# Expert weights loaded into the first mixer's own buffers, and normed rows stored from ScalarE's queue

## The chip, the cores and the metric

The kernel runs on one core of one Trainium2 chip. The metric is the device time of one execution in microseconds (us), lower is better; the time of before is the median of 3 runs.

## The reference, cut to what matters

Two layers over 512 latent and 256 context tokens of width 1024, all in float32. Layer 0 mixes by retention and by a gated linear recurrence, layer 1 by latent attention. Each layer then norms and modulates its rows, routes each token to 2 of 32 experts and runs these:

```python
h = modulate(rmsnorm(x, g), shift, scale)
e_flat, weights = router(h)                      # a group of 8 experts, then 2 in it
xin = h[row_tok].reshape(n_blocks, 128, 1024)    # the rows of each expert
yb = (silu(xin @ w_gate[e]) * (xin @ w_up[e])) @ w_down[e]
x = x + gate * y                                 # y: each token's two outputs, weighted and summed
```

An expert's `w_gate`, `w_up` and `w_down` are 2 MB each. All 32 experts' weights are read in each layer, whatever the routing.

## The kernel before, in words

Engines run their own instruction streams and meet on semaphores written out by hand. The program is a row of blocks; each ends with a barrier of all engines. Four stages matter here.

**Input projection** (`ab_project`) and **retention** (`retention`) of layer 0. They fill `rows` (four planes of 6 tiles by 512), `yT` (the recurrence's result, channels on partitions) and use `c.hT`. `retention` loads the output projection's weights into `w`, the two streams' gate rows (`load_gates`) and the rows of X.

**Output projection** (`ab_output`, tiles t = 0 to 5 of 128 tokens). PE computes two products of 512 columns per tile: half n of tile t is `recurrent` (L1099) plus `retained` (L1106), and its last matmul counts up `mm`. VectorE adds it, gated, to X (`add_gated`, L1143 and L1144). Of a finished tile, ScalarE takes the squares and the root (`square`, L159 and L162), VectorE scales the row (`scale`, L268), GpSimd adds the shift (`shift`, L277) and so finishes the normed row in `nh`, a ring of two tiles. PE transposes it (`transpose`, L290), ScalarE evicts one half (`first_half`, L299) and VectorE the other (`second_half`, L306) into `c.hT`, and PE computes the router's logits from there (`logits`, L226). SyncE's stream in this block is: the norm's gain, shift and scale rows, the router's weights, the first expert's gate and up weights (`load_early`, L1858), then `store` (L243): for each tile wait for `h_done`, store the normed row to `h_rows` in HBM, and at the end wait for both store semaphores (L246). `scale` of tile t waits for the store of tile t - 2.

**Routing and experts** (`experts`, with `routing`). VectorE and PE work out the lists of tokens, some 21 us, while PE fills its gaps with products that nobody reads (`turn_over`, L1723), 8, 14 and 12 instructions in the rows. After the list is done, GpSimd gathers the rows of experts 0, 1 and 2 from `h_rows` with indirect DMAs (L2121), for experts of more than 64 tokens all 128 rows. For each expert PE transposes the gathered rows (L2154), multiplies by gate and up (L2176 and L2177, or L2170 for an expert of at most 32 rows), ScalarE and VectorE form `h`, and PE transposes it and multiplies by down (L2217, L2219, L2211). ScalarE stores the output (L2269).

The weights have three slots (`SLOTS = 3`), each with a gate, an up and a down buffer. SyncE loads the rest of the three slots at the block's start: down 0, gate, up and down 1, gate and up 2, and, when the first gather has landed (`x_ready[0]`), down 2 (L1853). From then on a slot's next weights are loaded when PE has used it: `gate_up` waits for `gu_used`, `down` for `d_used`.

```python
for kind, q in w.rest[:-1]:
    w.load(sp, kind, q, q)
sp.wait_ge(x_ready[0], 16)
w.load(sp, *w.rest[-1], S - 1)
```

Layer 1 has the same output, routing and expert stages over its four latent tiles (`mla_output`), with four pieces loaded early.

Of the kernel before, what the change touches and what calls it, by code (L numbers as in the profile page):

```python
# [171 lines left out]
class NormModulate(RowNorm):  # L172
# [3 lines left out]
    def __init__(self, nc, c, a, s, layer, sub, t0, x_ready, h_out=None, sb=None, hT_free=None,  # L176
                 pairs=1, logits=None):
        sb = sb or s.sb
        super().__init__(nc, c, a, s, t0, x_ready, sb)
        self.layer, self.sub, self.h_out, self.hT_free = layer, sub, h_out, hT_free  # L180
        self.HB = 2
# [3 lines left out]
        self.pairs = pairs  # L185
        self.tp = [s.ps(f"ntp{i}", [P, 4, P]) for i in range(2 * pairs)]
        if logits is not None:
            self.lps = logits
            self.rw = sb("nrw", [P, KD, ROUTES])
            self.rb = sb("nrb", [P, ROUTES])  # L190
            self.rw_ready, self.lg_done, self.lg_out = (s.sem(n) for n in ("rw_ready", "lg_done", "lg_out"))
        self.m_ready, self.m_done, self.scaled, self.h_done, self.tr_done, self.ev_act, self.ev_dve = (
            s.sem(n) for n in ("norm_m_ready", "norm_m_done", "norm_scaled", "norm_h_done", "norm_tr_done", "norm_ev_act", "norm_ev_dve"))
        self.h_stored = [s.sem(f"norm_h_stored{i}") for i in range(self.HB)]
# [24 lines left out]
    def logits(self, pe, t):  # L219
# [5 lines left out]
        for k in range(KD):  # L225
            last = self.nc.tensor.matmul(self.lps[:, t, :], self.c.hT[:, k, t * P:(t + 1) * P], self.rw[:, k, :],  # L226
                                         start=(k == 0), stop=(k == KD - 1))
# [9 lines left out]
    def store(self, sp):  # L237

        if self.h_out is None:
            return  # L240
        for t in range(self.T):
            sp.wait_ge(self.h_done, t + 1)
            sp.dma_start(self.h_out[(self.t0 + t) * P:(self.t0 + t + 1) * P, :],  # L243
                         self.h[:, t % self.HB, :]).then_inc(self.h_stored[t % self.HB], 16)
        for i in range(self.HB):
            sp.wait_ge(self.h_stored[i], 16 * (self.T // self.HB))  # L246
# [13 lines left out]
    def scale(self, dve, link, t):  # L260
# [3 lines left out]
        if t >= self.HB:  # L264
            dve.wait_ge(self.tr_done, 2 * (t - self.HB) + 2)
            if self.h_out is not None:
                dve.wait_ge(self.h_stored[t % self.HB], 16 * (t // self.HB))
# [11 lines left out]
    def bank(self, t, half):  # L279
        return self.tp[2 * (t % self.pairs) + half]  # L280

    def transpose(self, pe, t):

        pe.wait_ge(self.h_done, t + 1)
        for half in range(2):
            if t >= self.pairs:
                pe.wait_ge(self.ev_dve if half else self.ev_act, t - self.pairs + 1)
            for j in range(4):
                k = 4 * half + j
                last = self.nc.tensor.transpose(self.bank(t, half)[:, j, :], self.h[:, t % self.HB, k * P:(k + 1) * P],  # L290
# [3 lines left out]
    def first_half(self, act, t):  # L294

        if t == 0 and self.hT_free:
            self.hT_free(act)
        act.wait_ge(self.tr_done, 2 * t + 1)
        self.nc.scalar.copy(self.c.hT[:, 0:4, t * P:(t + 1) * P], self.bank(t, 0)[:]).then_inc(self.ev_act, 1)  # L299

    def second_half(self, eng, t, copy=None):

        if t == 0 and self.hT_free:
            self.hT_free(eng)
        eng.wait_ge(self.tr_done, 2 * t + 2)
        (copy or self.nc.vector.tensor_copy)(self.c.hT[:, 4:8, t * P:(t + 1) * P], self.bank(t, 1)[:]).then_inc(self.ev_dve, 1)  # L306
# [26 lines left out]
def ab_project(nc, c, a, k, hT, rows, u, yT, space):  # L333


    with Scope(nc, "abp") as s:
# [14 lines left out]
        gw = s.sb("gw", [P, 2, LT, P])  # L351
# [8 lines left out]
        cs = s.sb("cs", [P, 2, NT - CT, RD // 2])  # L360
        L2 = (NT - CT) // 2
        t1 = s.sb("t1", [P, L2, RH, RD // 2])
# [14 lines left out]
        bias0, bias = gt[:, 0:512], s.sb("bias", [P, 512])  # L377
# [504 lines left out]
def retention(nc, c, a, k, rows, qT, kT, w, w_ready, gate, gate_ready, ms):  # L882
# [3 lines left out]
    with Scope(nc, "ret") as s:  # L886
# [1891 lines left out]
```

## Time and profile before

| | before |
|---|---|
| median of 3 runs | 2066.79 us (2065.3 to 2068.74) |
| the profiled execution | 2067.23 us |
| its span, first to last instruction | 2065.6 us |
| PE busy | 1719.8 us, 83% of the span |
| DMA moved | 559.64 MB, mean 271 GB/s |
| mean granted TensorE clock | 0.916 of full speed |

Times in the rows are counted from the start of the span. "Idle before" in brackets is what the engine waited for ahead of that instruction; an SPq row is a DMA issued from SyncE's queue, and what it lasts is the issue, not the transfer. A "clock" of 1.00 is the full 2.4 GHz, of 0.50 the lower level.

### The profile page before, as it was taken

What the parts mean: (1) busy time and instruction counts of PE and PEld (TensorE: products, weight loads), DVE (VectorE), ACT (ScalarE), POOL (GpSimd) and SP (SyncE); (2) the same over time, 40 slices, a digit from 0 to 9 for tenths busy, and PEclk for the clock granted to TensorE, in tenths of its full rate; (3) what the DMA queues carried; (4) which work ended last, traced back from release to release, by engine and by line L of the source; (5) the groups of instructions that cost most, each with busy time, mean ns of one, the idle gap of its engine ahead of it and who ended that gap; (6) DMA issues with size and microseconds to landing.
All of it is one profiled execution on the core that took longest, in us unless ns stands there. A gap on an engine that the chain in (4) does not pass through costs nothing. (4 is left out here: it accounts for less than half of the span.)

```text
span 2065.6 us, 26627 instructions
## 1 busy us (share of the span) xinstructions
PE 1719.8 (83%) x9184; PEld 874.9 (42%) x9185; DVE 679.7 (33%) x1211; ACT 438.4 (21%) x842; POOL 272.5 (13%) x393
## 2 busy tenths in 40 slices
PE   5999999899799799997538999999978899765561
PEld 3443344745344334443216445555534344333230
DVE  3403775643311111111124437775431111111115
ACT  3104443211001100111114125553101101101102
POOL 1002450311101100101013230000121000000001
PEclk9999999999899899999878999999979899878775
DMA  9877744530789999999962202001459999999994
GB/s 372 276 266 254 247 165 143 192 114 31 306 321 403 415 418 409 419 412 410 423 267 88 86 1 92 1 1 54 174 229 398 414 409 415 418 415 421 420 388 152
DMA packets 99608, 559.64 MB, mean 271 GB/s; under 512 B 17188, under 2 KB 37376, under 8 KB 59976
## 3 DMA queue, kind: packets, MB, share of 16 engines
q1 hardware_dynamic: 87152, 524.49, 63.9%
q0 software_dynamic: 7744, 20.98, 2.9%
q10 hardware_dynamic: 4632, 13.11, 1.7%
q8 instruction: 49, 0.80, 0.2%
q14 instruction: 31, 0.25, 0.0%
HBM read 522.88 MB, written 40.91 MB: 273 GB/s over the span
## 5 line engine op out<-in xcount | busy, mean ns | idle before, releaser
L2176 PE MATMUL exp_gps<-moew_wg,all_hT 128*64 128x512 f32 (+1 forms) x480 | 247.8, 642 | 45.9 <-DMA moew_wu<-in_moe_w_up 40.2
L2170 PE MATMUL exp_gps<-moew_wg,all_hT 128*32 128x256 f32 x1088 | 162.7, 466 | 134.4 <-DMA moew_wu<-in_moe_w_up 127.0
L2177 PE MATMUL exp_ups<-moew_wu,all_hT 128*64 128x512 f32 (+1 forms) x480 | 246.7, 639 | 0.0
L588 PE MATMUL abp_ps<-ab_w,all_hT 128*128 128x512 f32 x384 | 169.8, 597 | 0.6 <-PE abp_ps L588 0.3
L2170 PE MATMUL exp_ups<-moew_wu,all_hT 128*32 128x256 f32 x1088 | 162.4, 465 | 0.0
L2170 PEld LDWEIGHTS exp_gps<-moew_wg,all_hT 128*32 128x32 f32 x1088 | 72.7, 133 | 205.5 <-issue 178.6
L2176 PEld LDWEIGHTS exp_gps<-moew_wg,all_hT 128*64 128x64 f32 (+1 forms) x480 | 79.4, 171 | 175.2 <-issue 174.2
L2325 DVE TENSOR_TENSOR all_hT<-all_hT,exp_ups 64x512 f32<-64x512 f32 (+1 forms) x30 | 20.7, 690 | 366.1 <-ACT all_hT L2261 366.1
L2217 PE MATMUL exp_yps<-moew_wd,all_hT 128*64 128x512 f32 (+1 forms) x240 | 115.1, 596 | 0.2 <-issue 0.2
L2219 PE MATMUL exp_yps<-moew_wd,all_hT 128*64 128x512 f32 (+1 forms) x240 | 115.1, 596 | 0.0
L588 PEld LDWEIGHTS abp_ps<-ab_w,all_hT 128*128 128x128 f32 x384 | 71.4, 190 | 99.1 <-issue 97.5
L2323 DVE TENSOR_TENSOR all_hT<-all_hT,exp_ups 64x256 f32<-64x256 f32 x34 | 14.4, 425 | 286.7 <-ACT all_hT L2259 286.7
L2129 POOL COPY exp_idx<-all_tok 128x1 int32 (+1 forms) x58 | 10.4, 179 | 714.6 <-DVEq L2314 714.6
L2177 PEld LDWEIGHTS exp_ups<-moew_wu,all_hT 128*64 128x64 f32 (+1 forms) x480 | 80.2, 170 | 50.9 <-issue 50.9
L1450 PE MATMUL att_sc<-mlakv_KT,mlak_QT 96*128 96x384 f32 x256 | 99.0, 510 | 2.5 <-PEq L76 1.7
L2261 ACT ACTIVATE all_hT<-exp_gps 64x512 f32<-64x512 f32 (+1 forms) x30 | 17.8, 592 | 359.4 <-PE exp_ups L2177 359.4
L592 PE MATMUL abp_ps<-all_hT,ab_w 128*128 128x256 f32 (+1 forms) x256 | 89.9, 509 | 2.0 <-DMA ab_w<-in_ab_w_in 1.7
L2154 PE MATMUL exp_xps<-all_ident,all_hT 128*128 128x128 f32 x512 | 74.6, 289 | 12.0 <-issue 12.0
L2154 PEld LDWEIGHTS exp_xps<-all_ident,all_hT 128*128 128x128 f32 x512 | 64.4, 194 | 46.9 <-issue 46.9
L1522 DVE TENSOR_REDUCE att_nmax<-att_sc 128x1 f32<-128x768 f32 x64 | 61.2, 957 | 48.6 <-PE att_sc L1450 48.6
L2211 PE MATMUL exp_yps<-moew_wd,all_hT 128*32 128x256 f32 x1088 | 68.7, 395 | 8.4 <-DMA moew_wd<-in_moe_w_down 5.0
L2259 ACT ACTIVATE all_hT<-exp_gps 64x256 f32<-64x256 f32 x34 | 12.8, 375 | 289.2 <-PE exp_ups L2170 289.2
(428 smaller groups left out, 2566.4 us busy)
## 6 DMA issues: line engine op xcount, KB each, us to landing
moew_wg<-in_moe_w_gate SPq DMA_DIRECT2D x64, 2048.0 KB, 27.7
moew_wu<-in_moe_w_up SPq DMA_DIRECT2D x64, 2048.0 KB, 34.1
moew_wd<-in_moe_w_down SPq DMA_DIRECT2D x64, 2048.0 KB, 35.3
all_X<-in_ada_w SPq DMA_DIRECT2D x40, 1024.0 KB, 8.4
ys<-abp_zero SPq DMA_DIRECT2D x32, 448.0 KB, 8.8
ab_w<-in_ab_w_in SPq DMA_DIRECT2D x6, 2048.0 KB, 9.2
ab_rows<-in_ada_w SPq DMA_DIRECT2D x6, 1024.0 KB, 15.4
ys<-abp_zero SPq DMA_DIRECT2D x11, 512.0 KB, 6.8
```

What stands on the lines that cost most here:

```text
L588: last = nc.tensor.matmul(ps[i % RB][:], hT[:, kk, what * P:(what + 1) * P], w[n % S][:, kk, :], start=(kk == 0), stop=(kk == KD - 1))
L592: last = nc.tensor.matmul(ps[i % RB][:, 0:m], w[n % S][:, kk, ct * P:(ct + 1) * P], hT[:, kk, o:o + m], start=(kk == 0), stop=(kk == KD - 1))
L1450: last = nc.tensor.matmul(sc[n % 2][:, b, 0:HALF], k.QT[0:QD, h, t * P:(t + 1) * P], k.KT[0:QD, h, b * HALF:(b + 1) * HALF], start=True, s ...
L1522: V.tensor_reduce(nmax[:, n % R:n % R + 1], sc[n % 2][:, :, 0:HALF], mybir.AxisListType.XY, ALU.max, negate=True).then_inc(mx, 1)
L2154: last = nc.tensor.transpose(xps[k // 4][:, k % 4, :], x_by[q][:, k, :], c.ident[:])
L2170: last = nc.tensor.matmul(bank[lo + j * Q:lo + (j + 1) * Q, 0:HC], x[:, k, 0:Q], wt[:, k, j * HC:(j + 1) * HC], start=(k == 0), stop=(k == ...
L2176: nc.tensor.matmul(gps[0:rows, :], x[:, k, 0:rows], w.g[q][:, k, :], start=(k == 0), stop=(k == KD - 1))
L2177: last = nc.tensor.matmul(ups[at:at + rows, :], x[:, k, 0:rows], w.u[q][:, k, :], start=(k == 0), stop=(k == KD - 1))
L2211: last = nc.tensor.matmul(yps[j // 2][j * Q:(j + 1) * Q, 0:HC], hT[:, k, 0:Q], w.d[q][:, k, j * HC:(j + 1) * HC], start=(k == 0), stop=(k ...
L2217: nc.tensor.matmul(yps[0][0:rows, :], hT[:, k, 0:rows], w.d[q][:, k, 0:512], start=(k == 0), stop=(k == HT_N - 1))
L2219: last = nc.tensor.matmul(yps[1][at:at + rows, :], hT[:, k, 0:rows], w.d[q][:, k, 512:1024], start=(k == 0), stop=(k == HT_N - 1))
L2325: nc.vector.tensor_tensor(h[at:at + rows, :], sg[at:at + rows, :], ups[at:at + rows, :], ALU.mult).then_inc(h_done, 1)
```

## The change

What it does, part by part.

1. `rows`, `w`, `yT` and the recurrence's gate weights lie in one buffer `home`, 24,576 columns, which is six pieces of the size of an expert's matrix. A second buffer `room` (3 x 1024 columns) holds the retention tables first, then the gate rows and the router's weights, then the experts' output rows `y`. Both live until layer 0's experts are done.
2. Down 0 joins gate 0 and up 0 in `load_early`.
3. When the last product is done (`mm` at 12), SyncE loads five more pieces into `home`: gate 1, up 1 and down 1 over `w` and `yT`, gate 2 and up 2 over planes of `rows`.
4. The last piece, down 2, is loaded in the experts' block, when all six normed rows have landed in HBM (`rows_stored`), since these lie in its place until they are stored.
5. The normed rows of layer 0 are stored from ScalarE's queue, each between the tile's successor's `square` and its own `first_half`. No engine waits for the stores at the end of the block; GpSimd does so (`rows_stored`) before the first gather. In layer 1 SyncE still stores them, and GpSimd awaits them too.
6. The gate rows are loaded at the start of `ab_output`, no longer in `retention`, and VectorE waits for them ahead of `add_gated`.
7. The transposed normed rows go to a ring of two tiles in `c.hT`, whose rest holds the shift and scale rows; `first_half` and `second_half` of tile t wait for the logits of tile t - 2.

The diff, cut:

```diff
 def store(self, eng, t):
-        if self.h_out is None:
-            return
-        for t in range(self.T):
-            sp.wait_ge(self.h_done, t + 1)
-            sp.dma_start(...).then_inc(self.h_stored[t % self.HB], 16)
-        for i in range(self.HB):
-            sp.wait_ge(self.h_stored[i], 16 * (self.T // self.HB))
+        eng.wait_ge(self.h_done, t + 1)
+        eng.dma_start(self.h_out[(self.t0 + t) * P:(self.t0 + t + 1) * P, :],
+                      self.h[:, t % self.HB, :]).then_inc(self.h_stored[t % self.HB], 16)
...
     def first_half(self, act, t):
+        if t >= self.ring:
+            act.wait_ge(self.lg_done, t - self.ring + 1)
         act.wait_ge(self.tr_done, 2 * t + 1)
...
 # retention
             sp.dma_start(w, a["ab_w_out"][0].rearrange("(k p) n -> p k n", p=P)).then_inc(w_ready, 16)
-            load_gates(sp, c, gate, gate_ready, 0, 0, 2)
             load_rows(sp, c, a, [c.x_ready] * NT)
-            sp.wait_ge(gate_ready, 32)
...
 # ab_output
         @block.sync
         def _(sp):
+            load_gates(sp, c, gate, gate_ready, 0, 0, 2)
             norm.load(sp)
             norm.load_router(sp)
             ew.load_early(sp)
-            norm.store(sp)
+            sp.wait_ge(mm, 2 * NT)
+            ew.load_freed(sp)
...
             for t in range(NT):
                 norm.square(act, t)
                 if t >= 1:
+                    norm.store(act, t - 1)
                     norm.first_half(act, t - 1)
+            norm.store(act, NT - 1)
             norm.first_half(act, NT - 1)
...
             dve.wait_ge(c.x_ready, 16 * NT)
+            dve.wait_ge(gate_ready, 32)
...
 # ab_layer
-        ew = ExpertWeights(nc, a, 0, [("g", 0), ("u", 0)])
+        pieces = [home[:, i * PIECE:(i + 1) * PIECE] for i in range(6)]
+        ew = ExpertWeights(nc, a, 0, [("g", 0), ("u", 0), ("d", 0)],
+                           [("g", 1, pieces[3]), ("u", 1, pieces[4]), ("d", 1, pieces[5]),
+                            ("g", 2, pieces[2]), ("u", 2, pieces[1])], ("d", 2, pieces[0]), room)
...
+    def load_freed(self, sp):
+        for kind, q, _space in self.freed:
+            self.load(sp, kind, q, q)
+
+    def rows_stored(self, eng, tiles):
+        for stored in self.h_stored:
+            eng.wait_ge(stored, 16 * (tiles // 2))
...
 # experts, sync
-            for kind, q in w.rest[:-1]:
-                w.load(sp, kind, q, q)
-            sp.wait_ge(x_ready[0], 16)
-            w.load(sp, *w.rest[-1], S - 1)
+            if w.late:
+                w.rows_stored(sp, NT - t0)
+                w.load(sp, *w.late[0:2], S - 1)
+            else:
+                ...
...
 # experts, gpsimd
             pool.wait_ge(xg_set, S)
+            w.rows_stored(pool, NT - t0)
             pool.wait_ge(route.listed, 1)
```

How this moves the DMAs, at the two places of which the prediction speaks. First SyncE's queue from the first expert's weights in the output block to the start of the experts' loop; `moew_w*` are expert weights at places of their own, `home_pieces` the buffer of part 1, and the branches are the end of the output block and the start of the experts'. Before:

```order
L1858 DMA moew_wg<-in_moe_w_gate 128x4096
L1858 DMA moew_wu<-in_moe_w_up 128x4096
L243 DMA h_rows<-ab_rows 128x1024 x6
L73 UNCONDITIONAL_BRANCH
L2079 UNCONDITIONAL_BRANCH
L1853 DMA moew_wd<-in_moe_w_down 128x2x2048
L1858 DMA moew_wg<-in_moe_w_gate 128x4096
L1858 DMA moew_wu<-in_moe_w_up 128x4096
L1853 DMA moew_wd<-in_moe_w_down 128x2x2048
L1858 DMA moew_wg<-in_moe_w_gate 128x4096
L1858 DMA moew_wu<-in_moe_w_up 128x4096
L1853 DMA moew_wd<-in_moe_w_down 128x2x2048
```

And now:

```order
L1873 DMA moew_wg<-in_moe_w_gate 128x4096
L1873 DMA moew_wu<-in_moe_w_up 128x4096
L1868 DMA moew_wd<-in_moe_w_down 128x2x2048
L1873 DMA home_pieces<-in_moe_w_gate 128x4096
L1873 DMA home_pieces<-in_moe_w_up 128x4096
L1868 DMA home_pieces<-in_moe_w_down 128x2x2048
L1873 DMA home_pieces<-in_moe_w_gate 128x4096
L1873 DMA home_pieces<-in_moe_w_up 128x4096
L73 UNCONDITIONAL_BRANCH
L2102 UNCONDITIONAL_BRANCH
L1868 DMA home_pieces<-in_moe_w_down 128x2x2048
```

Six of the seven loads that stood behind the block's end now stand ahead of it, and the six stores are gone from this queue.

Second, ScalarE at the end of the output block, its last two tiles. Before:

```order
L159 ACTIVATE ab_rows,abo_nms<-all_X 128x1024
L162 ACTIVATE abo_nroot<-abo_nms,abo_neps 128x1
L299 COPY all_hT<-abo_ntp 128x4x128 x2
L73 UNCONDITIONAL_BRANCH
L2241 UNCONDITIONAL_BRANCH
```

And now:

```order
L159 ACTIVATE home_pieces,abo_nms<-all_X 128x1024
L162 ACTIVATE abo_nroot<-abo_nms,abo_neps 128x1
L238 DMA h_rows<-home_pieces 128x1024
L288 COPY all_hT<-abo_ntp 128x4x128
L238 DMA h_rows<-home_pieces 128x1024
L288 COPY all_hT<-abo_ntp 128x4x128
L73 UNCONDITIONAL_BRANCH
L2269 UNCONDITIONAL_BRANCH
```

A store's issue now stands ahead of each eviction. PE, VectorE and GpSimd have the same instructions in the same order as before.

## Rows read from the trace of the kernel before

**Rows 1.** The page: span, and GB/s in 40 equal slices of 51.6 us

```profile
span 2065.6 us, 26627 instructions
...
GB/s 372 276 266 254 247 165 143 192 114 31 306 321 403 415 418 409 419 412 410 423 267 88 86 1 92 1 1 54 174 229 398 414 409 415 418 415 421 420 388 152
```

**Rows 2.** Timeline of SyncE's queue, 350 to 760 us: start, length, line, out<-in

```profile
409.49 4.41 SPq L216 DMA_DIRECT2D abo_nrb<-in_moe_group_b  x1
...
414.90 0.43 SPq L1858 DMA_DIRECT2D moew_wu<-in_moe_w_up  x1
...
519.74 0.40 SPq L1853 DMA_DIRECT2D moew_wd<-in_moe_w_down  x1
...
522.41 0.45 SPq L1858 DMA_DIRECT2D moew_wu<-in_moe_w_up  x1
553.24 0.38 SPq L1853 DMA_DIRECT2D moew_wd<-in_moe_w_down  x1
572.38 0.33 SPq L1858 DMA_DIRECT2D moew_wg<-in_moe_w_gate  x1
```

**Rows 3.** Timeline of all engines around the first gather and the first expert

```profile
539.25 7.09 PE L1723 MATMUL exp_yps<-all_X,all_ident 128*128 128x512 f32 x12
...
541.69 1.22 POOL L2121 DMA_INDIRECT all_hT<-h_rows,all_tok  x1 [18.23 <-issue]
...
553.32 1.95 PE L2154 MATMUL exp_xps<-all_ident,all_hT 128*128 128x128 f32 x8 [6.97 <-issue]
...
556.49 2.07 PE L2176 MATMUL exp_gps<-moew_wg,all_hT 128*128 128x512 f32 x2 [1.23 <-DVE all_hT L2315]
...
561.02 1.02 PE L2177 MATMUL exp_ups<-moew_wu,all_hT 128*128 128x512 f32 x2
...
572.18 1.05 PE L2154 MATMUL exp_xps<-all_ident,all_hT 128*128 128x128 f32 x8
```

**Rows 4.** Windows of 2 us: length, busy PE, PEld, DVE, ACT, POOL, clock, DMA, GB/s

```profile
550.00:552.00 2.00, 0.00 (x0) 0.00 (x0) 0.00 (x0) 0.00 (x0) 0.00 (x0) 0.51 0.95 365
...
562.00:564.00 2.00, 2.00 (x6) 0.83 (x5) 0.00 (x0) 0.00 (x0) 0.00 (x0) 1.00 0.00 0
...
578.00:580.00 2.00, 2.00 (x24) 1.05 (x20) 0.00 (x0) 0.00 (x0) 0.00 (x0) 0.50 1.02 424
```

**Rows 5.** DMA by queue, 547 to 549 us: packets, MB, share of 16 engines

```profile
q1 hardware_dynamic: 50, 0.79, 92.7%
q0 software_dynamic: 50, 0.11, 14.0%
```

**Rows 6.** Gathers issued at 541.7, 1527.7, 2026.7, 1067.3: median us to landing

```profile
all_hT<-h_rows,all_tok POOLq DMA_INDIRECT x1, 11.5
...
all_hT<-h_rows,all_tok POOLq DMA_INDIRECT x1, 6.2
...
comb_y<-ys,all_slot POOLq DMA_INDIRECT x2, 4.9
...
comb_y<-ys,all_slot POOLq DMA_INDIRECT x2, 7.4
```

**Rows 7.** Timeline of all engines, the end of the output block

```profile
500.06 3.60 PE L1106 MATMUL abo_ps<-ab_w,ab_rows 128*128 128x512 f32 x8
...
506.53 0.57 ACT L299 COPY all_hT<-abo_ntp 128x512 f32<-128x512 f32 x1
...
507.15 1.98 PE L226 MATMUL abo_tp<-abo_nrw,all_hT 128*128 128x36 f32 x16 [0.91 <-ACT all_hT L299]
...
511.55 0.32 SPq L243 DMA_DIRECT2D h_rows<-ab_rows  x1
...
514.41 3.60 PE L226 MATMUL abo_tp<-abo_nrw,all_hT 128*128 128x36 f32 x16 [0.88 <-DVE all_hT L306]
```

**Rows 8.** ScalarE's issues of the experts' outputs: ns min/median/max, first and last start

```profile
L2269 ACTq DMA_DIRECT2D ys<-exp_y x64: 321/327/580, 591.4 to 2021.6; - x64
```

**Rows 9.** VectorE's first gated product of the output block

```profile
428.38 0.69 DVE L1143 TENSOR_TENSOR ab_rows<-abo_ps,ab_gate 128x512 f32<-128x512 f32 x1 [10.84 <-PE abo_ps L1106]
```

More of the change, by code:

```diff
@@ L184, in __init__, with columns @@
         self.h = sb("nh", [P, self.HB, DM])
[L185 to L191, printed above, removed]
+        self.tp = [s.ps(f"ntp{i}", [P, 4, P]) for i in range(2)]
+        self.lps = logits
+        self.rw = sb("nrw", [P, KD, ROUTES])
+        self.rb = sb("nrb", [P, ROUTES])
+        self.rw_ready, self.lg_done, self.lg_out = (s.sem(n) for n in ("rw_ready", "lg_done", "lg_out"))
         self.m_ready, self.m_done, self.scaled, self.h_done, self.tr_done, self.ev_act, self.ev_dve = (
             s.sem(n) for n in ("norm_m_ready", "norm_m_done", "norm_scaled", "norm_h_done", "norm_tr_done", "norm_ev_act", "norm_ev_dve"))
-        self.h_stored = [s.sem(f"norm_h_stored{i}") for i in range(self.HB)]
+    def columns(self, t):
+        return slice(t % self.ring * P, (t % self.ring + 1) * P)
     def load(self, sp):
@@ L330, in load_rows, with ab_project @@
         eng.dma_start(c.X[:, t, :], rows).then_inc(ready[t], 16)
-def ab_project(nc, c, a, k, hT, rows, u, yT, space):
+def ab_project(nc, c, a, k, hT, rows, u, yT, space, gw, rest):
     with Scope(nc, "abp") as s:
@@ L359, in ab_project @@
         zero = s.sb("zero", [P, DM // 4])
[L360 removed]
+        part = carve(rest)
+        cs = part("cs", [P, 2, NT - CT, RD // 2])
         L2 = (NT - CT) // 2
[L362 removed]
+        t1 = part("t1", [P, L2, RH, RD // 2])
         t2 = gt[:, 0:L2 * RH * RD // 2].rearrange("p (t h n) -> p t h n", t=L2, h=RH)
@@ L1017, in _, with ab_output @@
                 sum_squares(t)
-def ab_output(nc, c, a, gate, rows, yT, w, w_ready, ms, ew):
+def ab_output(nc, c, a, room, rows, yT, w, w_ready, ms, ew):
     with Scope(nc, "abo") as s:
@@ L1569, in _ @@
             ew.load_early(sp)
-            norm.store(sp)
+            for t in range(L):
+                norm.store(sp, t)
         @block.tensor
@@ L1836, in __init__ @@
         self.d_ready = [self.scope.sem(f"d_ready{i}") for i in range(SLOTS)]
+        self.h_stored = [self.scope.sem(f"h_stored{i}") for i in range(2)]
         self.place(early)
+        for kind, q, space in (*freed, *([late] if late else [])):
+            self.buf[kind, q] = space.rearrange("p (k n) -> p k n", k=HT_N if kind == "d" else KD)
     def place(self, pieces):
@@ L1844, in place_rest @@
     def place_rest(self):
-        self.rest = [(kind, q) for q in range(SLOTS) for kind in "gud" if (kind, q) not in self.early]
+        self.rest = [(kind, q) for q in range(SLOTS) for kind in "gud" if (kind, q) not in self.buf]
         self.place(self.rest)
@@ L2080, in _ @@
         def _(sp):
-            for kind, q in w.rest[:-1]:
-                w.load(sp, kind, q, q)
-            sp.wait_ge(x_ready[0], 16)
-            w.load(sp, *w.rest[-1], S - 1)
+            if w.late:
+                w.rows_stored(sp, NT - t0)
+                w.load(sp, *w.late[0:2], S - 1)
+            else:
+                for kind, q in w.rest[:-1]:
+                    w.load(sp, kind, q, q)
+                sp.wait_ge(x_ready[0], 16)
+                w.load(sp, *w.rest[-1], S - 1)
             def gate_up(n, q):
```

121 lines of the change are left out of this document (64 added, 57 removed).

## The prediction

> **What bounds the kernel now.** I began with the page's slices of DMA throughput [rows 1]. In both expert loops, slices 12 to 19 and 30 to 37 (counted from 0), DMA runs at some 400 to 420 GB/s: the loops live on the stream of weights. In between lie slices with almost none, and slice 9, 465 to 516 us, with 31 GB/s, is the end of layer 0's output block. A megabyte moved into that hole looks free. The question is what it buys, so I read next which event starts the stream for good.
>
> SyncE's queue shows it [rows 2]. Six pieces, 12.6 MB, are issued from 519.74 to 522.9 us, the seventh at 553.24 when the first gather has landed, and then nothing until 572.38. From there each load follows the use of a slot. In 562 to 564 us DMA moves nothing [rows 4]: all nine pieces are there and the queue waits for expert 0's gate and up products. So the stream's real start is not the loading of the pieces but the end of expert 0's gate and up, and that follows from the gather.
>
> The timeline around it [rows 3]: GpSimd issues gather 0 at 541.69. PE's last filler products end at 539.25 + 7.09 = 546.34. The gathered rows come 11.5 us after their issue [rows 6], and PE starts their transposes at 553.32, after 6.97 us of idleness. The DMA queues tell why the gather is slow: in 547 to 549 us the weights' queue moves 0.79 MB and the gather's 0.11 MB [rows 5]. The loads of 519.74 to 522.9 take 12.6 MB at 415 GB/s, 30 us, to about 550, and the gather crawls until they are out of the way.
>
> **The change, part by part.** All against the profiled execution, 2067.23 us; its span is 2065.6.
>
> *Loads moved ahead.* The last product runs at 500.06 + 3.60 = 503.7 us [rows 7]. Then SyncE issues five pieces, 10.5 MB, 25 us at 415 GB/s, done at about 529. Down 0 goes with gate 0 and up 0, after 414.90 [rows 2], into nearly empty DMA. Down 2 waits for the stores and takes 5 us more. No load of the three slots is then in flight at 541.69.
>
> *First term, the gather.* On idle DMA it should land in 4.9 us, as in the last stage, against 11.5 now and 6.2 in layer 1, where four pieces are still draining; in the combine of layer 0, beside the gate rows' loads, it was 7.4 [rows 6]. I take 4.9, because only that gather starts with as empty a queue. 541.69 + 4.9 = 546.6, just behind PE's fillers (546.34). Transposes start at 546.7 instead of 553.3: **-6.6 us**. Bounds: -7.0 (PE free at 546.34) and -4.2 (7.4 us).
>
> *Second term, TensorE's clock.* While PE idles before the gather the granted clock falls to the lower level, 0.51 in 550 to 552 us [rows 4]. The transposes then take 1.95 us where expert 1's at 572.18 take 1.05 [rows 3], and the first three of 16 groups of products take 561.02 - 556.49 = 4.53 us, where a group at the full clock takes (572.18 - 561.02) / 13 = 0.86, so 2.58. Without the idle 7 us both should run at 1.00: -0.9 and -1.95, **-2.9 us**. Bounds: 0, if the 3 us with only transposes still let the clock fall, as it stands at 0.50 in 578 to 580 after the thin stretch behind expert 0 [rows 4]; and -4.6, if that later fall is spared too (some 3.5 us at half rate, 1.7). I take -2.9, since PE's break is now 0.4 us, a transpose, and about 1.5 us.
>
> *From there on nothing is left to win.* At the end of expert 0's gate and up all nine pieces are in place in either kernel and DMA is idle. The loads of expert 3 start then, and every later one hangs on PE's use of a slot. The chain moves forward as a whole; the 30 us of transfer that were moved buy no more than these terms. Routing takes as long as before: its work is on VectorE and PE.
>
> *Stores from ScalarE.* ScalarE issued 64 stores among heavy loads in 0.32 to 0.58 us [rows 8]. Ahead of the eviction at 506.53 such an issue delays logits that start at 507.15 and last 2 us, and PE needs nothing more before tile 5's row at 511.6. Tile 5's store is issued at about 511.6 while PE transposes, and the eviction that follows is not the late one: PE waits for VectorE's half before 514.41 [rows 7]. Cost 0. Upper bound: SyncE has an issue of 4.41 us behind others [rows 2]. Twice that on ScalarE would end the logits of tile 4 at 513.6 and move 514.41 to about 516.9: +2.5. `scale` of tile t waits for the store of tile t - 2, which is now issued one tile later, some 16 us before it is needed.
>
> *Awaiting the stores at the gather.* Tile 5's store now travels beside the five pieces. It lands between 514.2 (2.6 us, unhindered) and about 532 (as gather 0 did, 3 us after the loads are through). Both ends lie before 541.69, and down 2 behind it ends by 537. Cost 0. Queued behind the wait on GpSimd are only the gathers, behind the one on SyncE only down 2 and the loop, which has nothing to do before expert 0.
>
> *Gate rows a block later.* 1 MB more ahead of the shift and scale rows, at 400 to 250 GB/s 2.5 to 4 us later. VectorE has 10.84 us of idleness before its first gated product [rows 9]. Cost 0; without that cover, 4 us.
>
> *The ring of two tiles in hT* waits for logits that PE issues ahead of the transposes which the same eviction waits for: 0. *Layer 1*: GpSimd awaits stores that landed long before: 0.
>
> **Sum.** -6.6 - 2.9 = -9.5 us, 2067.23 - 9.5 = 2057.7. The median of before lies 0.4 below its profiled execution, so I forecast **2057.3 us** as the median.
>
> **The rivals.**
>
> *A: part of it is eaten.* The gather lands in 6 to 7.4 us, the clock falls anyway, or ScalarE's issue stalls for 2.5: between -1.7 and -6, about 2062.5 us. For it: rows 6 spread, and the clock falls after many thin stretches. Against it: each needs a cause that the idle DMA takes away.
>
> *B: the gather's 11.5 us are its own.* If the queues shared DMA by halves, gather 0 would need 2.5 us for its 0.5 MB beside the loads instead of 1.3, and the loads would explain 1.3 us of the 11.5; the rest would stay, with PE's idleness and its clock: 2065.5 us. Against it stand 4.9 us elsewhere and the split of 0.79 to 0.11 MB. The Trainium skill has the rule (DMA: Bandwidth & Descriptors, section on queues, rings and completion order): each DMA engine goes round the queues packet by packet. By that rule with equal packets we would be in B; the trace agrees with the turns (50 packets each) and shows the packets unequal, 16 KB against 2.
>
> *C: the bytes count in full.* If the loop were bound by DMA from its first byte, 30 us of transfer gone would save up to 30: 2037. The idle DMA of 562 to 564 us speaks against it.
>
> *D: slower, by the wait for the stores.* Down 2 and gather 0 both wait for tile 5's row. Both are let go by the same event; a gather issued into down 2's transfer needs 5 us more. With the row in HBM at S, expert 0 starts at S + 5 + 4.9 + 0.1. It is later than now from S = 543.3 on. With the store held up until 3 us after the five pieces, that takes 10.5 MB from 503.7 to 540.3: 287 GB/s or less. At 250 GB/s, as in slices 3 and 4 [rows 1], S = 548.7 and the start is at 558.7: +5.4, 2072 us. Against it: the same source and kind of load runs at 415 in the loop, and slices 3 and 4 hold smaller transfers.
>
> **How the numbers follow.** About 0.2% of the time, 4.1 us, is what a measurement here can tell from no change. Forecast 0.73, A 0.13, B 0.05, C 0.04, D 0.05. The forecast's own range is 2055 to 2060.5. From its lower end I go down to 2053, for the later fall of the clock and the spread of runs; upward to 2063, which takes in most of A. Left out are B, C, D and the rest of A, under 0.2. Faster: the forecast, C and most of A, 0.87; within 0.2%: B and the rest of A, 0.08; slower: D, 0.05.
>
> **What would show it right or wrong.** Five loads on SyncE's queue at about 504 us, through by 530; gather 0 issued at 541.7 and landed in about 5 us; transposes of expert 0 at about 546.7 in 1.05 us; the next slot's load at about 563 instead of 572.38, and every later stage earlier by the same 9 to 10 us. It is wrong if gather 0 starts late (D), lands in over 8 us (B), if the clock stands at 0.50 around 550 us (A), if an ACTq store lasts more than 1 us, or if the difference grows or shrinks by more than 2 us between 575 us and the end of the loop.

## The result, and the profile after

| | before | after |
|---|---|---|
| median, same chip | 2067.79 us (2065.3 to 2073.2, 5 runs) | 2055.21 us (2052.52 to 2057.47, 5 runs) |
| ratio, 95% interval | | 0.9936 [0.9922, 0.9949] |
| the profiled execution, its span | 2067.23, 2065.6 us | 2053.72, 2052.0 us |
| PE busy | 1719.8 us | 1720.2 us |

The kernel is faster, by 10.5 to 16 us (0.5 to 0.8%). The forecast was 9.5 us and a time of 2057.3 us. The page of the kernel after, GB/s in 40 slices of 51.3 us:

```profile
span 2052.0 us, 26634 instructions
...
GB/s 371 272 296 235 268 160 144 168 157 140 216 358 406 418 411 417 416 417 410 425 244 90 39 7 87 1 1 96 142 278 399 411 416 414 412 415 421 420 359 149
```

The hole of slice 9, 31 GB/s before [rows 1], holds 140 GB/s now, and slice 10 has sunk from 306 to 216: transfer was moved ahead. What it bought is in the timeline. SyncE's and ScalarE's queues of the kernel after, 496 to 557 us (start, length, line, out<-in), answer to [rows 2, 7, 8]:

```profile
496.44 0.33 SPq L1873 DMA_DIRECT2D home_pieces<-in_moe_w_gate  x1
...
498.55 0.47 SPq L1873 DMA_DIRECT2D home_pieces<-in_moe_w_up  x1
...
504.31 0.33 ACTq L238 DMA_DIRECT2D h_rows<-home_pieces  x1
...
514.27 0.38 SPq L1868 DMA_DIRECT2D home_pieces<-in_moe_w_down  x1
...
556.99 0.33 SPq L1873 DMA_DIRECT2D moew_wg<-in_moe_w_gate  x1
```

Five loads go out in 2.6 us behind the last product. Tile 5's row is stored at 504.31, and down 2 follows at 514.27, when the row is in HBM. The next load follows expert 0's gate and up, at 556.99 instead of 572.38. Around the first gather, against [rows 3]:

```profile
532.75 8.09 PE L1735 MATMUL exp_yps<-all_X,all_ident 128*128 128x512 f32 x12
...
535.26 1.22 POOL L2149 DMA_INDIRECT all_hT<-h_rows,all_tok  x1 [18.97 <-issue]
...
540.68 1.05 PE L2182 MATMUL exp_xps<-all_ident,all_hT 128*128 128x128 f32 x8
...
542.97 1.12 PE L2204 MATMUL exp_gps<-moew_wg,all_hT 128*128 128x512 f32 x2 [1.24 <-DVE all_hT L2343]
...
556.80 1.05 PE L2182 MATMUL exp_xps<-all_ident,all_hT 128*128 128x128 f32 x8
```

The transposes start 5.42 us behind the gather's issue, before it was 11.63. They last 1.05 us instead of 1.95 and have no idleness ahead of them: the fillers end with the landing. The landing of gather 0 and windows (length, busy PE, PEld, DVE, ACT, POOL, clock, DMA, GB/s) of the kernel after, against [rows 4, 6]:

```profile
all_hT<-h_rows,all_tok POOLq DMA_INDIRECT x1, 4.9
```

```profile
520.00:530.00 10.00, 8.17 (x33) 4.47 (x31) 8.57 (x23) 0.00 (x0) 0.00 (x0) 1.00 1.01 426
530.00:540.00 10.00, 10.00 (x32) 5.94 (x32) 2.26 (x9) 0.00 (x0) 3.18 (x3) 0.66 0.24 68
550.00:552.00 2.00, 2.00 (x6) 0.88 (x5) 0.00 (x0) 0.00 (x0) 0.00 (x0) 1.00 0.03 8
...
562.00:564.00 2.00, 2.00 (x28) 1.04 (x24) 0.00 (x0) 0.00 (x0) 0.00 (x0) 0.52 0.94 401
```

All transfers are through before the gather is issued, the clock at 550 us is 1.00 instead of 0.51 (and 1.00 in 540 to 542 too, where the transposes run), and the later fall of the clock, behind expert 0, is still there (0.52 in 562 to 564).

Since the program up to the gather's issue also ran earlier, I read each stage against the event that opens it:

| | before | after | gain |
|---|---|---|---|
| gather 0 issued | 541.69 | 535.26 | 6.4 |
| from there to the end of expert 0's gate and up | 30.49 | 21.54 | 8.95 |
| from there to the combine of layer 0 (its first load) | 494.40 | 494.05 | 0.35 |
| from there to the final norm's load | 966.28 | 968.51 | -2.2 |

The last row shows no effect of the change. From the combine on the time is 967.25 and 970.31 us in the two other traces of the old layout, 968.04 and 967.73 in the two others of the change.

The 8.95 us are the two terms of the forecast (9.5). From the end of expert 0's gate and up, layer 0 runs through its 31 other experts in the same time within 0.4 us. What is over is the 6.4 us ahead of the gather, for which the forecast had nothing. In these two traces part of that lies at one spot in the input projection, where PE waits 3.2 to 3.3 us for `all_X<-in_ada_w` in both and then goes on. Timeline of PE before:

```profile
127.88 1.93 PE L547 MATMUL abp_aps<-all_X,abp_sT 128*32 128x512 f32 x8 [3.32 <-DMA all_X<-in_ada_w]
129.74 9.03 PE L592 MATMUL abp_ps<-all_hT,ab_w 128*128 128x512 f32 x16
```

and after:

```profile
126.61 1.06 PE L536 MATMUL abp_aps<-all_X,abp_sT 128*32 128x512 f32 x8 [3.18 <-DMA all_X<-in_ada_w]
127.60 7.13 PE L581 MATMUL abp_ps<-all_hT,home_pieces 128*128 128x512 f32 x16
```

The same 24 matmuls behind the same idleness take 10.9 us at a clock that has fallen, and 8.1 us at one that has not. The new layout alone doesn't decide this: in x12, another trace of the changed kernel, the clock fell here too and they take 11.0 us.

### The profile page after: what moved, and what is told of

Its sections match the earlier page's. It is cut to its first block and busy times, and to the rows that moved or that the text cites. A ratio compares the mean times of both kernels' runs of the same rounds, so it can differ in the third digit from the quotient of the medians.

```text
span 2052.0 us, 26634 instructions
## 1 busy us (share of the span) xinstructions
PE 1720.2 (84%) x9184; PEld 875.8 (43%) x9185; DVE 679.7 (33%) x1211; ACT 439.6 (21%) x842; POOL 272.4 (13%) x393
## 5 line engine op out<-in xcount | busy, mean ns | idle before, releaser
L577 PE MATMUL abp_ps<-home_pieces,all_hT 128*128 128x512 f32 x384 | 169.8, 597 | 0.6 <-PE abp_ps L581 0.3
L2204 PE MATMUL exp_gps<-moew_wg,all_hT 128*64 128x512 f32 (+1 forms) x272 | 137.8, 642 | 28.7 <-DMA moew_wu<-in_moe_w_up 24.3
L2205 PE MATMUL exp_ups<-moew_wu,all_hT 128*64 128x512 f32 (+1 forms) x272 | 136.6, 638 | 0.0
L2204 PE MATMUL exp_gps<-home_pieces,all_hT 128*128 128x512 f32 (+1 forms) x208 | 108.8, 635 | 22.2 <-DMA home_pieces<-in_moe_w_up 20.9
L577 PEld LDWEIGHTS abp_ps<-home_pieces,all_hT 128*128 128x128 f32 x384 | 71.4, 190 | 99.1 <-issue 97.5
L2205 PE MATMUL exp_ups<-home_pieces,all_hT 128*128 128x512 f32 (+1 forms) x208 | 107.8, 630 | 0.0
L581 PE MATMUL abp_ps<-all_hT,home_pieces 128*128 128x256 f32 (+1 forms) x256 | 87.2, 497 | 2.0 <-DVE all_hT L734 1.7
L2204 PEld LDWEIGHTS exp_gps<-moew_wg,all_hT 128*64 128x64 f32 (+1 forms) x272 | 42.9, 163 | 102.7 <-issue 102.1
L2204 PEld LDWEIGHTS exp_gps<-home_pieces,all_hT 128*128 128x128 f32 (+1 forms) x208 | 36.1, 179 | 75.3 <-issue 74.8
L2149 POOL DMA_INDIRECT all_hT<-h_rows,exp_idx x58 | 56.6, 975 | 80.2 <-issue 80.2
```

The costliest lines, as they stand in the source:

```text
L577: last = nc.tensor.matmul(ps[i % RB][:], hT[:, kk, what * P:(what + 1) * P], w[n % S][:, kk, :], start=(kk == 0), stop=(kk == KD - 1))
L581: last = nc.tensor.matmul(ps[i % RB][:, 0:m], w[n % S][:, kk, ct * P:(ct + 1) * P], hT[:, kk, o:o + m], start=(kk == 0), stop=(kk == KD - 1))
L2149: nc.gpsimd.indirect_dma_start(xg[q][0:rows, :], None, c.h_rows[:, :], bass.IndirectOffsetOnAxis(index[0:rows], 0), bounds_check=TOK - 1, ...
L2204: nc.tensor.matmul(gps[0:rows, :], x[:, k, 0:rows], w.g[q][:, k, :], start=(k == 0), stop=(k == KD - 1))
L2205: last = nc.tensor.matmul(ups[at:at + rows, :], x[:, k, 0:rows], w.u[q][:, k, :], start=(k == 0), stop=(k == KD - 1))
```

## The experiments

Theories: **T**, the forecast's two terms (a quick gather, and TensorE's clock kept) make the gain. **P**, it is the earlier stream of weights itself. **Q**, it is the stores' move to ScalarE. Ratios are against runs of before on the same chip, whose medians were 2065.94 to 2068.05 us.

Of the profiled executions: start of expert 0's transposes, their length, end of its gate and up, and layer 0's combine, all but the length counted from gather 0's issue. The runs were made on several chips, so medians are best compared by their ratios, and a trace is one execution, which can lie anywhere among its kernel's.

| kernel | median us | ratio [95%] | transposes | length | gate, up end | combine |
|---|---|---|---|---|---|---|
| before | 2067.79 | | 11.63 | 1.95 | 30.49 | 524.89 |
| after | 2055.21 | 0.9936 [0.9922, 0.9949] | 5.42 | 1.05 | 21.54 | 515.59 |
| x1 places only | 2064.24 | 0.9989 [0.9979, 0.9999] | 12.96 | 1.95 | 32.85 | 524.55 |
| x2 before, filled | 2063.95 | 0.9981 [0.9966, 0.9995] | 12.49 | 1.94 | 31.00 | 525.51 |
| x3 gather first | 2071.02 | 1.0020 [1.0009, 1.0030] | 4.95 | 1.14 | 21.15 | 532.12 |
| x4 stores on SyncE | 2055.70 | 0.9950 [0.9936, 0.9963] | 4.83 | 1.13 | 21.03 | 513.55 |
| x5 three early | 2055.18 | 0.9939 [0.9927, 0.9952] | 4.48 | 1.13 | 20.68 | 514.29 |
| x6 no last fillers | 2057.62 | 0.9941 [0.9928, 0.9955] | 5.06 | 1.94 | 23.78 | 518.52 |
| x7 gate first | 2060.06 | 0.9957 [0.9945, 0.9970] | 5.06 | 1.13 | 21.26 | 517.96 |
| x8 after again | 2055.12 | 0.9935 [0.9915, 0.9955] | 4.81 | 1.93 | 23.67 | 517.75 |
| x9 gate first, 128 rows | 2051.68 | 0.9933 [0.9912, 0.9954] | 5.37 | 1.13 | 23.27 | 511.79 |
| x10 two more fillers | 2053.98 | 0.9937 [0.9921, 0.9953] | 7.17 | 1.05 | 23.29 | 518.43 |
| x11 x9 again | 2049.59 | 0.9922 [0.9904, 0.9940] | 5.51 | 1.05 | 21.62 | 509.24 |
| x12 after, third | 2056.71 | 0.9949 [0.9937, 0.9962] | 5.15 | 1.13 | 21.35 | 514.94 |

### x1: the new places, the loads as before

```diff
 # ab_output, sync
-            ew.load_early(sp)
-            sp.wait_ge(mm, 2 * NT)
-            ew.load_freed(sp)
+            for kind, q in ew.early[0:2]:
+                ew.load(sp, kind, q, q)
 # experts, sync
-                w.rows_stored(sp, NT - t0)
+                w.load(sp, "d", 0, 0)
+                w.load_freed(sp)
+                sp.wait_ge(x_ready[0], 16)
                 w.load(sp, *w.late[0:2], S - 1)
```

> The change's buffers, its stores from ScalarE and its waits, but the weights are loaded when they were before: gate 0 and up 0 in the output block, down 0 and the five pieces at the start of the experts' block, down 2 after the first gather. Theory G (the gain is gather 0 that no longer travels beside loads, and TensorE's clock behind it): gather 0 lands again in 11 to 12 us, the transposes of expert 0 take about 1.95 us at half clock, and the time is that of before, 2067, within 2. Rival L (the new places, the moved gate rows or the stores from ScalarE save some 3 us by themselves, which would be the part of the gain that the sum did not have): 2064 or less, with the output block shorter than before's 115.6 us in its profile.

Measured 2064.24, a gain of 2.3 us (0.2 to 4.3) where the change has 13. That lies between what the theory expected (2065 to 2069) and the rival (2064 or less). The gather crawls again; DMA by queue in 546 to 548 us of x1:

```profile
q1 hardware_dynamic: 49, 0.80, 94.6%
q0 software_dynamic: 48, 0.09, 11.7%
```

These are the shares of [rows 5]. So what is gained from the gather on comes from the loads' times alone. The buffers, the ScalarE stores, the later waits and the gate rows cost nothing, and 2.3 us of the gain come with them, as far as 12 executions can tell.

### x3: before, with all loads behind the gather

```diff
 # experts, sync
+            if layer == 0:
+                sp.wait_ge(x_ready[0], 16)
             for kind, q in w.rest[:-1]:
```

> The kernel before, but in layer 0 SyncE waits for the first gather ahead of the six loads, which then go with the seventh. Theory G: gather 0 lands in about 5 us on idle DMA, the transposes start at about 546.7 in 1.05 us and expert 0's gate and up end at about 563, as in the change. What the early loads are worth by themselves is then read from the total: seven pieces, 14.7 MB or 35 us, start at 546.6 and end at 582, and the loads of expert 3 queue behind them instead of starting at 572.4; if the loop is bound by the stream from there, 2070 to 2075, slower than before although expert 0 is early. Rival P (PE's path alone sets the loop, so the bytes need not be moved): 2057, as the change.

Expert 0 is as early as in the change (its gate and up end 21.15 us behind the gather), and yet layer 0's combine is 7.2 us later than before, in an execution that was the slowest of twelve (2076.29); by the ratio x3 is 4 us slower than before (2 to 6). The loads go out from 547.45 to 551.53, and from there DMA has no pause: in 580 to 600 us PE already stands and waits for weights. From the end of expert 0's gate and up to the combine it takes 511.0 us, where before took 494.4. A quick gather is worth nothing if it is bought with the stream. The change is the way to have both.

### x4: the stores on SyncE's queue

```diff
 # ab_output, sync
             ew.load_early(sp)
+            for t in range(NT - 1):
+                norm.store(sp, t)
             sp.wait_ge(mm, 2 * NT)
             ew.load_freed(sp)
+            norm.store(sp, NT - 1)
 # ab_output, scalar: both norm.store calls gone
```

> The change, but the normed rows are stored from SyncE's queue again: tiles 0 to 4 ahead of the wait for the last product, tile 5 behind the five loads. Theory G: the store of tile 5 lands only when the loads are through, at about 522 to 527 by the change's times, down 2 follows and is in place by 532, gather 0 at 535 still finds idle DMA: the time of the change, 2055 within 2. Rival Q (the queue matters: the row must be ahead of the loads, or ScalarE's queue is what saves time in the output block): 2058 or more, with gather 0 issued late or landed in over 6 us.

The queue of the stores makes no difference that can be measured (Q falls). SyncE's queue of x4 shows how long tile 5's row stays behind five pieces, since down 2 waits for it:

```profile
502.95 0.44 SPq L1874 DMA_DIRECT2D home_pieces<-in_moe_w_up  x1
508.61 0.33 SPq L238 DMA_DIRECT2D h_rows<-home_pieces  x1
530.08 0.38 SPq L1869 DMA_DIRECT2D home_pieces<-in_moe_w_down  x1
```

21 us from issue to landing, and still 9 us ahead of the gather, so nobody waits. From ScalarE's queue it took 9.9 us. That margin is what the move of the stores buys here.

### x5: three pieces early instead of six

```diff
             sp.wait_ge(mm, 2 * NT)
-            ew.load_freed(sp)
+            for kind, q, _space in ew.freed[0:2]:
+                ew.load(sp, kind, q, q)
 # experts, sync
+                for kind, q, _space in w.freed[2:]:
+                    w.load(sp, kind, q, q)
                 w.rows_stored(sp, NT - t0)
```

> The change, but only down 0, gate 1 and up 1 are loaded early; down 1, gate 2 and up 2 go at the start of the experts' block, at about 513, and down 2 behind them once the rows are stored. Theory G: these four pieces, 8.4 MB, 20 us, are through at about 533, just ahead of gather 0 at 535, so half of the moved bytes give the whole gain: 2055 to 2056. Rival P2 (each moved byte counts): half of the gain, 2061.

Down 0, gate 1 and up 1 ahead, the rest from 517.07 on, through when the gather is issued at 539.06: the whole gain. Of the pieces moved, half are enough to clear the way; P, by which each earlier piece counts, falls.

### x2: before, with fillers until the gather has landed

```diff
         last.then_inc(list_done, 1)
-        turn_over(6)
+        turn_over(14 if layer == 0 else 6)
```

> The kernel before with fourteen last filler groups instead of six in layer 0, so that TensorE works on until its first tokens have landed; nothing else differs, the gather still runs beside the weight loads. It prices the clock alone. Theory (the clock gives back what the forecast put at 2.9 us, besides what the gather gives): first transposes about 553 in 1.05 us instead of 1.95, gate and up products of expert 0 at full clock, the next slot's load about 27.6 us behind the gather's issue instead of 30.5, 2063.5 us in all (ratio 0.9985). Rival (the half clock costs nothing by itself, because a later wait takes it up, or the fillers overrun the landing): no change or a loss of up to 1 us, 2066.5 to 2067.5.

Inconclusive as a price of the clock. The fillers ended at 552.46, but this gather landed later still. PE stood 2.67 us, and the clock fell all the same. Windows of x2:

```profile
552.00:554.00 2.00, 0.46 (x2) 0.00 (x0) 0.00 (x0) 0.00 (x0) 0.00 (x0) 1.00 0.71 232
554.00:556.00 2.00, 0.88 (x4) 0.91 (x5) 0.00 (x0) 0.00 (x0) 0.00 (x0) 0.63 0.39 131
556.00:558.00 2.00, 1.07 (x6) 0.67 (x4) 0.69 (x1) 0.59 (x1) 0.36 (x2) 0.50 0.92 229
```

Its median is 4 us under before, as expected, with executions from 2057.9 to 2072.8. But the trace is of the slowest of the twelve, and expert 0 gained nothing in it. Whether the clock held in the faster ones is not known, so the median can't be put down to the clock.

### x6 and x10: no last fillers, two more

```diff
-        turn_over(6)
+        turn_over(0 if layer == 0 else 6)      # x6
+        turn_over(8 if layer == 0 else 6)      # x10
```

> The changed kernel without the last six filler groups of layer 0. TensorE then stands idle for some 8 us before the first transposes. Theory: the transposes can start no earlier than the gather's landing plus the checks on it, 0 to 1 us earlier than in the changed kernel, but the clock has fallen by then, and transposes (1.95 us) and the first groups cost 2.9 us more: the changed kernel plus 2 to 3 us, 2057.5 to 2058.5. Rival (the fillers are what the transposes wait for, and they cost more than they keep): the changed kernel less 0.5 to 2 us, 2053.5 to 2055.

> The changed kernel with eight last filler groups instead of six in layer 0, 1.7 us more work, so that TensorE is still busy when the first rows have landed (in one profiled run of the changed kernel the six ended 1.9 us before the transposes, which then ran in 1.93 us, in the other they ended with them and the transposes took 1.05 us). Theory (the gap decides the clock): transposes in 1.05 to 1.15 us right behind the fillers, next slot's load 21.5 to 22.5 us behind the gather's issue, 0 to 1.5 us under the changed kernel, 2053.5 to 2055. Rival (the fillers now end last and the transposes wait for them): 0.5 to 1.5 us over it, 2055.5 to 2056.5.

In x6 PE idles 7.36 us, the transposes start at the landing, and with the clock down gate and up end 23.78 us behind the gather instead of 21.35 to 21.54 in the two traces of the change whose clock held: the clock is worth 2.3 us. In x10 the fillers end last, 7.17 us behind the gather's issue, the clock holds, and it ends at 23.29: what the fillers keep they cost. So x10's median, 2053.98, fell where its theory had it, but its trace shows the rival's mechanism. Both medians lie within 2.5 us of x8's, on the same program otherwise; with executions that spread over 9 us and more, no difference of the times can be claimed. Of x6's 2.5 us, 1 lies outside the program: its times exceed their spans by 2.0 to 3.4 us, those of the other kernels by 1.7, and the medians of the spans are 1.5 apart.

### x7: gate products first, and the next gate piece loaded behind them

```diff
 # experts, sync, gate_up
-                sp.wait_ge(gu_used, n + 1)
+                sp.wait_ge(g_used, n + 1)
                 w.load(sp, "g", n + S, q)
+                sp.wait_ge(gu_used, n + 1)
                 w.load(sp, "u", n + S, q)
 # experts, PE, up (more than 32 rows)
                     for k in range(KD):
-                        nc.tensor.matmul(gps...)
+                        last = nc.tensor.matmul(gps...)
+                    last.then_inc(g_used, 1)
+                    for k in range(KD):
                         last = nc.tensor.matmul(ups...)
```

(For experts of at most 32 rows, left out here, `g_used` is counted up at the last products, so nothing moves there.)

> The changed kernel with expert's gate products all ahead of its up products (where it has more than 32 rows) and a semaphore of their own, so that the next slot's gate piece is loaded when the gate products are done and not when both are, some 7 us earlier. In the changed kernel the DMA stands still for about 8 us (548 to 556) while expert 0 multiplies, and after it TensorE waits for weights in the rest of the layer. Theory (from there on the layer is bound by its stream of weights, so each us by which the stream starts earlier comes off in full): 4 to 7 us less in layer 0 and as much or less in layer 1, 2043 to 2050 us. Rival 1 (what was forecast: nothing left to win from an earlier stream once TensorE has started): the same as the changed kernel, 2054 to 2056. Rival 2 (gate and up products interleaved share their stationary tile, apart they load it twice): slower than the changed kernel by 3 us or more.

Slower than the change by about 5 us, though DMA ran earlier: PE is busy for 511 us in 500 to 1060, against 474 in the change. The cause is in the experts of 64 rows. Timeline of PE, one such expert in the change:

```profile
817.16 0.64 PE L2204 MATMUL exp_gps<-home_pieces,all_hT 128*64 128x512 f32 x1
817.16 0.64 PE L2205 MATMUL exp_ups<-home_pieces,all_hT 128*64 128x512 f32 x1
817.64 0.59 PE L2204 MATMUL exp_gps<-home_pieces,all_hT 128*64 128x512 f32 x1
817.64 0.59 PE L2205 MATMUL exp_ups<-home_pieces,all_hT 128*64 128x512 f32 x1
```

and one in x7:

```profile
829.81 5.79 PE L2207 MATMUL exp_gps<-home_pieces,all_hT 128*64 128x512 f32 x13
835.02 0.64 PE L2210 MATMUL exp_ups<-home_pieces,all_hT 128*64 128x512 f32 x1
...
836.36 5.74 PE L2210 MATMUL exp_ups<-home_pieces,all_hT 128*64 128x512 f32 x13
```

A gate and an up product of 64 columns, side by side in the code and in different halves of the output's partitions, start at the same instant: 16 pairs take 7.0 us. Parted they overlap only in three, and take 12.2 us. The size is that of rival 2, the reason is another: each product loads its stationary tile in either order (for 480 gate products of these experts 480 loads, and as many for up, in the change and in x7).

### x9 and x11: gate first for experts of 128 rows alone

```diff
 # as x7, but in PE's up
+                        if rows < P:
+                            last = nc.tensor.matmul(ups...)   # interleaved as in the change
+                    if rows == P:
+                        for k in range(KD):
+                            last = nc.tensor.matmul(ups...)
```

> Gate products ahead of up products only for experts of 128 rows; the experts of 64 rows keep the two interleaved, since the profile of the run that parted them shows gate and up of 64 rows taking 12.2 us one after the other where interleaved they take 7.0 us. Theory (once TensorE has started, the layer's time is set from its last gap in the DMA on, and a gate piece loaded 6 to 7 us earlier beside that gap closes part of it): 2 to 5 us under the changed kernel, 2050 to 2053, and from 540 to 620 us fewer idle microseconds of DMA. Rival (what was forecast: an earlier transfer buys nothing behind TensorE's start): the changed kernel's time, 2054.5 to 2056. Second rival (the semaphore of its own and SyncE's two waits cost more than they give): over 2057.

> The same kernel as x9_gate_first_full (gate products first for experts of 128 rows only), again, beside the changed kernel on one chip, since its six executions ran from 2046.0 to 2060.7 us and its ratio could not be told from the changed kernel's. Theory (the gate piece loaded 7 us earlier closes part of the last gap of the weight stream, which in the profile moved layer 0's combine from about 516 to 518 us behind the gather to 512): 2050 to 2053, 2 to 5 us under the changed kernel. Rival (no gain behind TensorE's start): within 1.5 us of the changed kernel.

> The changed kernel itself again, on the same chip as the three beside it, to see how much of the 3 us beyond the forecast holds. Theory (the profile's extra 4 us of the first stage and 3 us of the output block are the runs' own spread, and the change is worth its two terms and the small gain of the layout): 2055 to 2057, 10 to 12 us under the kernel before. Rival (the change is worth 13 us or more in every run): 2052 to 2054.

> The changed kernel a third time, beside x11_gate_first_again: 2054 to 2057 us. In its trace the combine of layer 0 comes 515 to 518 us behind the gather's issue, as in the two profiled runs of it so far (515.6 and 517.8).

The two repetitions of the change gave 2055.12 and 2056.71, as expected. x9's own ratio could not be told from the change's; with its repetition it can. Twelve executions of this kernel have a mean of 2050.9 us, the 17 of the change in three sets 2056.0: 5.0 us less, 95% interval 1.9 to 8.2. Against x12 on its own chip x11 has 6.8 less (2 to 12). The trace shows where. Windows of x12, the change:

```profile
580.00:600.00 20.00, 20.00 (x84) 9.77 (x83) 2.98 (x6) 1.91 (x4) 1.31 (x3) 1.00 0.79 315
600.00:620.00 20.00, 20.00 (x77) 9.74 (x79) 2.67 (x4) 1.77 (x3) 1.41 (x3) 1.00 0.96 388
```

and of x11:

```profile
580.00:600.00 20.00, 20.00 (x84) 9.77 (x83) 2.82 (x5) 1.91 (x4) 1.31 (x3) 1.00 0.99 404
600.00:620.00 20.00, 20.00 (x105) 10.01 (x107) 2.67 (x4) 1.77 (x3) 1.41 (x3) 1.00 0.92 348
```

PE is busy throughout in both; only DMA has work where it paused. Later, where PE waits for weights, it pays. Waits of PE for gate and up weights in 540 to 1060 us (line, waited for, us in total, times, longest), x12:

```profile
PE exp_gps L2198 <- DMA home_pieces<-in_moe_w_up: 21.8, 4, 9.5
PE exp_gps L2204 <- DMA home_pieces<-in_moe_w_up: 18.3, 4, 8.2
PE exp_gps L2198 <- DMA moew_wu<-in_moe_w_up: 9.6, 3, 6.1
...
PE exp_gps L2204 <- DMA moew_wu<-in_moe_w_up: 5.1, 1, 5.1
```

and x11:

```profile
PE exp_gps L2199 <- DMA home_pieces<-in_moe_w_up: 20.0, 3, 9.5
PE exp_gps L2207 <- DMA home_pieces<-in_moe_w_up: 19.0, 4, 7.5
PE exp_gps L2199 <- DMA moew_wu<-in_moe_w_up: 8.9, 2, 7.2
...
PE exp_gps L2207 <- DMA moew_wu<-in_moe_w_up: 2.3, 1, 2.3
```

54.8 us against 50.2, and the combine 5.7 us earlier from the gather. From the end of expert 0's gate and up to the combine it takes 488.5 and 487.6 us in x9 and x11, and 493.6 to 494.1 in the three traces of the change. That is layer 0. In layer 1, which the edit also touches, 963.8 and 963.3 us from the combine to the final norm's load stand against 967.7 to 968.5; but x4, whose layer 1 is that of the change, has 962.7, so a gain there is not shown. The two traces are of fast executions (2046.40 of 2046.04 to 2060.68, and 2044.55, the fastest of its six). This is the fastest kernel of the study, about 17 us (0.8%) under before.

## Why the prediction was right, and where it was not

Seventeen executions of the change have a mean of 2056.0 us and 67 of before 2067.5: a gain of 11.6 us, 95% interval 10.0 to 13.1. The forecast was 9.5, at 2057.3. That it came so near is in part luck: its two terms brought 8.3 us in the mean of the three traces of the change, and 2 to 3 us came from the stages ahead of the gather, for which it had nothing.

*What bounds.* Right. x3 and x5 show both halves of it: the gather's landing decides when expert 0 starts, and the transfers need only be out of its way and not behind PE.

*First term, the gather: -6.6.* Landing in 4.9 us, as taken. The transposes start 4.48 to 5.51 us behind the gather's issue in all runs with an idle DMA and the fillers of the change, instead of 11.63: -6.2 in the profiled pair, -6.5 in the mean of the three traces of the change. In the profiled execution the fillers, not the rows, ended last.

*Second term, the clock: -2.9.* Found in the profiled pair as 8.95 - 6.2 = 2.75. But it is not certain: in x8, the same program, the fillers ended 1.9 us ahead of the transposes, these took 1.93 us, and the end of gate and up came 18.86 us behind the start of the transposes, exactly as before, where it came 16.12 us behind in the first trace and 16.20 in x12. So this term is 0 or 2.7 us, by the execution, 1.8 in the mean of the three. The step "PE's break is now 0.4 us" leaned on one trace for when the fillers end; they run now at one clock, now at the other (5.40 us in x8, 8.09 in the first trace). Of the sum, this is the term that is too large.

*Nothing left to win from there on.* Right for the pieces moved: between the end of gate and up and the combine it took 494.4 us before and 493.6 to 494.1 in the three traces of the change. As a general sentence it is wrong. I argued that every later load hangs on PE's use of a slot, and did not look at the next pauses of DMA, in 580 to 620 us, behind which PE is the one that waits. Gate pieces issued some 6 us earlier there, and behind every other expert of 128 rows in both layers, were worth 5 us in all (x9, x11).

*Stores from ScalarE, awaiting them, gate rows, the ring: 0 each.* No cost, by x1 and x4. VectorE's first gated product still waits for PE, 4.74 us instead of 10.84, so the later gate rows stayed under cover. The stores' issues last 0.33 to 0.37 us, none stalls, and the row lands 10 us after its issue, within the 2.6 to 20 us given. Had it stayed in SyncE's queue it would have landed at 530, by x4.

*Ahead of the gather: 0 forecast.* This is the term that is missing. The gather was issued at 541.69, 542.63 and 542.57 us in the three profiled executions of the old layout and at 535.26 to 542.95, on average 538.7, in the eleven of the new one. x1's 2.3 us lie here, and with 8.8 from the gather to the combine (mean of the three traces of the change) they give 11.1 of the 11.6 measured. Most of the spread of that part follows the clock at two spots that have the same work in all: in 120 to 140 us it was 0.83 in all three old ones, in the new 0.83 four times, 0.91 four times, 1.00 three times; the first stage ends at 351.2 to 352.5 us where it was 1.00, and at 354.7 to 357.7 where it was 0.83. And the output block's first 32 products took 16.9 to 17.0 us in the old ones; in the new 14.0 twice, 15.7 twice and 16.9 to 17.0 seven times. The trace of the change shown above has the best of both, 1.00 and 13.97; x12, the same program, has 0.83 and 16.93, and issues its gather at 540.00. So the 6.4 us of the profiled pair are not the change's own figure. Whether the new layout makes a high clock likelier there, which would be x1's 2.3 us, or whether fourteen profiles are too few is open. No run here tells, and the code up to 350 us differs only in where its buffers lie.

*The rivals.* A fell as a whole, though its clock appears in one of three traces of the change (x8). B fell: quiet queues land the gather in 4 to 5 us. In x1 49 packets move 0.80 MB and 48 packets 0.09. The Trainium skill's rule of turns packet by packet (DMA: Bandwidth & Descriptors, section on queues, rings and completion order) agrees with these counts; the unequal packets make the crawl of it. C fell by the time itself, 2055 and not 2037, and by x5. D fell: 10.5 MB were through by 530 and the row landed at 514, 21 us ahead of the gather; even the 530 of x4 left 9.

## What to carry to other kernels

Before moving a transfer ahead, ask which short transfer runs beside it and who waits for that; here 12 MB of weights mattered only by standing in the way of half a megabyte of rows. Then look for the last pause of the big stream ahead of the place where the compute engine starts to wait for it: here loads made possible 6 us earlier there gave 5 us (1.9 to 8.2), and 30 us of transfer moved ahead of earlier pauses gave nothing beyond the gather and its clock. And of kernels whose clock falls in thin stretches, profile the same one several times before putting 3 us down to the change.

## What the runs showed of the hardware that I had not expected

The granted clock behind one and the same idleness differs between executions of one program. In the three traces of the change PE waits 3.18, 3.26 and 3.05 us for `in_ada_w`; the 24 matmuls behind took 8.1 us in the first two (clock 1.00 in 120 to 140 us) and 11.0 in the third (0.83). After 1.89 us of idleness it fell in x8. After 0.75 us in x9 the transposes ran at the full rate (1.13 us), but in 546 to 548 the clock was 0.50, and the sixteen gate products behind them took 8.82 us where they took 7.13 in x7.

Two matmuls of 64 stationary columns that are neighbours in the stream and write to different halves of the partitions run at the same time: 7.0 us for 16 pairs, against 12.2 when they are parted.
